# Two hybrid blocks on one core: retention scores one step further behind the rotation, and the gate pieces of two outputs beside the last head

## The reference, cut to what matters

```python
q = rotary(q, positions)
k = rotary(k, positions) * (dk ** -0.5)
...
att = jnp.einsum('bhnd,bhmd->bhnm', qc, kc) * inner_decay
...
mu = jnp.mean(out, axis=-1, keepdims=True)
var = jnp.mean(jnp.square(out - mu), axis=-1, keepdims=True)
out = (out - mu) * lax.rsqrt(var + EPS)
...
y_ret = o_ret.astype(x.dtype) * jax.nn.silu(zr)
merged = jax.nn.sigmoid(ga) * (y_att @ w_proj_attn) + jax.nn.sigmoid(gr) * (y_ret @ w_proj_ret)
return x + gate[:, None, :] * (merged @ w_out)
```

## Time and profile before

| | us |
|---|---|
| median of 3 runs | 3543.75 |
| lowest and highest | 3541.46, 3548.41 |
| the profiled execution's own time | 3547.39 |
| its span | 3545.6 |
| PE busy | 3335.2 (94%) |
| DVE busy | 1714.1 (48%) |
| ACT busy | 1287.0 (36%) |
| POOL busy | 409.7 (12%) |

### The profile page before, as it was taken

The page is one execution under the profiler, slowest core; times in us unless marked ns, Lnnn a source line. Parts: engine busy times, 40 slices in busy tenths (PEclk is TensorE's granted clock), DMA queues, the critical chain, the costliest instruction groups (busy, mean ns, idle before and its releaser), DMA issues.

```text
span 3545.6 us, 42895 instructions
## 1 busy us (share of the span) xinstructions
PE 3335.2 (94%) x17064; PEld 2755.8 (78%) x17064; DVE 1714.1 (48%) x2596; ACT 1287.0 (36%) x1991; POOL 409.7 (12%) x400
## 2 busy tenths in 40 slices
PE   3999998999998999988999999999999999999898
PEld 3788777888887788876888778877778788877686
DVE  3666568655524667676333333343333333433333
ACT  2555533212123656563322333333332333333322
POOL 1111110000001445352000000001200000021100
PEclk7999999999998999999999999999999999999999
DMA  5222224665512111111333322222123222222132
GB/s 178 87 75 81 73 76 135 193 199 185 183 55 69 49 42 48 48 42 63 97 98 97 102 80 71 72 81 74 63 78 98 91 77 72 66 89 78 51 97 85
DMA packets 109286, 318.75 MB, mean 90 GB/s; under 512 B 28192, under 2 KB 30880, under 8 KB 108576
## 3 DMA queue, kind: packets, MB, share of 16 engines
q1 hardware_dynamic: 109088, 316.00, 28.3%
HBM read 313.86 MB, written 2.10 MB: 89 GB/s over the span
## 4 chain that ended last, share of the span: by engine, by line
PE 82%; DVE 7%; ACT 4%; POOL 3%; issue 2%; DMA 1%; SPq 0%; DVEq 0%; ACTq 0%
PE bank L1013 21%; PE bank L1015 20%; PE bank L1014 20%; PE bank L1018 3%; PE bank L1019 3%; PE bank L1020 3%; PE bank L1225 1%; PE bank L1099 1%; DVE tmp L1694 1%; PE bank L1244 1%; PE bank L1109 1%; PE bank L1254 1%; PE bank L1126 1%; ACT L1282 1%; POOL hg_d L2142 1%
## 5 line engine op out<-in xcount | busy, mean ns | idle before, releaser
L1013 PE MATMUL bank<-h_high_lat,w_high 128*128 128x512 f32 x2742 | 1139.8, 416 | 96.4 <-DVE h_low_ctx L1700 34.1
L1642 DVE TENSOR_TENSOR w_low<-w_raw,w_high 128x1024 fp32r<-128x1024 f32 (+3 forms) x442 | 539.8, 1223 | 1135.3 <-ACT w_high L1302 1134.3
L1015 PE MATMUL bank<-h_high_lat,w_low 128*128 128x512 f32 x2742 | 1082.2, 395 | 0.0
L1014 PE MATMUL bank<-h_low_lat,w_high 128*128 128x512 f32 x2742 | 1081.7, 395 | 0.0
L1302 ACT CAST w_high<-w_raw 128x1024 fp32r<-128x1024 f32 (+3 forms) x442 | 451.4, 1022 | 1304.5 <-PE bank L1015 845.7
L1013 PEld LDWEIGHTS bank<-h_high_lat,w_high 128*128 128x128 f32 x2742 | 522.8, 191 | 220.4 <-issue 83.1
L1015 PEld LDWEIGHTS bank<-h_high_lat,w_low 128*128 128x128 f32 x2742 | 522.1, 190 | 113.7
L1014 PEld LDWEIGHTS bank<-h_low_lat,w_high 128*128 128x128 f32 x2742 | 524.4, 191 | 79.5 <-issue 8.3
L2096 POOL TENSOR_TENSOR rstd<-rstd,square 128x512 f32<-128x512 f32 (+1 forms) x42 | 64.8, 1544 | 1456.6 <-ACT square L1283 1455.7
L1018 PE MATMUL bank<-h_high_ctx,w_high 128*128 128x256 f32 x795 | 224.8, 283 | 0.0
L1019 PE MATMUL bank<-h_low_ctx,w_high 128*128 128x256 f32 x795 | 224.7, 283 | 0.0
(11 more groups left out here) (264 smaller groups left out, 4378.9 us busy)
## 6 DMA issues: line engine op xcount, KB each, us to landing
w_raw<-in_w_in_dram SPq DMA_DIRECT2D x176, 512.0 KB, 3.5
w_raw<-in_ada_w_dram SPq DMA_DIRECT2D x88, 512.0 KB, 4.0
w_raw<-in_ffn_in_dram SPq DMA_DIRECT2D x88, 512.0 KB, 3.5
w_raw<-in_w_ada_dram SPq DMA_DIRECT2D x48, 512.0 KB, 4.4
w_raw<-in_hg_in_dram SPq DMA_DIRECT2D x40, 512.0 KB, 3.5
w_raw<-in_ffn_out_dram SPq DMA_DIRECT2D x32, 512.0 KB, 3.5
w_raw<-in_qkv_dram SPq DMA_DIRECT2D x24, 512.0 KB, 3.6
w_raw<-in_proj_ret_dram SPq DMA_DIRECT2D x16, 512.0 KB, 3.5
```

The lines of the kernel that those rows point to most:

```text
L1013: e.matmul(lat_b, a, h[:, k, :], start=start, stop=False)
L1014: e.matmul(lat_b, a, l[:, k, :], start=False, stop=False)
L1015: done = e.matmul(lat_b, b, h[:, k, :], start=False, stop=stop)
L1642: e.tensor_tensor(w_lo[n % 2][:, 0:w], raw[slot][:, 0:w], w_hi[n % 2][:, 0:w].bitcast(F32), ALU.subtract).then_inc(s_lo, 1)
```

## The change

1. `re_mixer` gets an empty step between the rotation and the first scores: 11 steps for 10.
2. The pieces beside the last head are ga(0), gr(0), pa(0), ga(1), gr(1) in 31 slots, with pa(1) behind; before they were ga(0) and gr(0) in 14 slots, with pa(0) behind.
3. In the merge the gates run one output ahead: pr(0), then ga(2), gr(2), pa(2), pr(1), and so on to ga(7), gr(7), pa(7), pr(6), pr(7).
4. `merge_gate` has four buffers for two, and the waits for a free one look one output further back.

```diff
--- before.py
+++ after.py
@@ -394,6 +394,7 @@
             self.ev("re_vt", x, c)
         self.ev("re_rot", x)
         yield
+        yield
         for jt in range(4):
             self.ev("re_sc", x, jt)
             yield
@@ -505,19 +506,20 @@
             first = self.re_mixer(layer, 0)
             start_first = []
             self.interleave([self.at_pieces(layer, j) for j in range(ATT_H)], [(self.at_mixer(layer, j), 7) for j in range(ATT_H)],
-                            10 * (KC - 1), self.re_pieces(layer, 0, lambda: self.start_background(first, 10, 8 * (KC - 1))), 5 * (KC - 1))
+                            10 * (KC - 1), self.re_pieces(layer, 0, lambda: self.start_background(first, 11, 8 * (KC - 1))), 5 * (KC - 1))
             for k in range(ATT_H):
                 self.ev("ya", layer, k)
             self.preload()
             self.ev("re_init", layer)
             self.interleave([self.re_pieces(layer, r) for r in range(1, RET_H)],
-                            [(self.re_mixer(layer, r), 10) for r in range(1, RET_H)], 8 * (KC - 1), self.gate_pieces(layer, 0), 2 * (KC - 1))
+                            [(self.re_mixer(layer, r), 11) for r in range(1, RET_H)], 8 * (KC - 1),
+                            self.gate_pieces(layer, 0) + self.gate_pieces(layer, 1), 4 * (KC - 1) + ATT_H - 1)
             self.preload()
             for k in range(KC):
                 self.ev("yr", layer, k)
             for m in range(KC):
-                if m > 0:
-                    for p in self.gate_pieces(layer, m):
+                if 0 < m < KC - 1:
+                    for p in self.gate_pieces(layer, m + 1):
                         p()
                 self.piece(io["proj_ret"][layer, m], KC, "yr", ("pr", layer, m), gate=("yr", layer) if m == 0 else None)
             for m in range(KC):
@@ -611,7 +613,7 @@
         with ExitStack() as sy:
             YR = sb("y_ret", [P, KC, LAT], F32, sy)
             YAh, YAl = sb("ya_high", [P, ATT_H, LAT], F32R, sy), sb("ya_low", [P, ATT_H, LAT], F32R, sy)
-            gates2 = ring("merge_gate", 2, [P, LAT], sy)
+            gates2 = ring("merge_gate", 4, [P, LAT], sy)
             with ExitStack() as si:
                 head_in = ring("head_in", 14, [P, LAT], si)
                 with ExitStack() as st:
@@ -1417,12 +1419,12 @@
                     elif what == "gate":
                         _, name, layer, m = p.epi
                         g = KC * layer + m
-                        if g > 0 and name == "ga":
-                            e.wait_ge(*lat_free[by_epi[("pa", *divmod(g - 1, KC))]])
-                        elif g > 0:
-                            e.wait_ge(s_ma, g)
+                        if g > 1 and name == "ga":
+                            e.wait_ge(*lat_free[by_epi[("pa", *divmod(g - 2, KC))]])
+                        elif g > 1:
+                            e.wait_ge(s_ma, g - 1)
                         e.wait_ge(s_mm, n + 1)
-                        act(gates2[0 if name == "ga" else 1][:, :], lat_b, ACT.Sigmoid).then_inc(s_la, 1)
+                        act(gates2[2 * (m % 2) + (name == "gr")][:, :], lat_b, ACT.Sigmoid).then_inc(s_la, 1)
                     elif what == "pr":
                         _, layer, m = p.epi
                         e.wait_ge(s_ma, KC * layer + m + 1)
@@ -1777,10 +1779,10 @@
                             e.wait_ge(s_ml, KC * layer + m - 1)
                         e.wait_ge(*lat_free[by_epi[("gate", "ga", layer, m)]])
                         e.wait_ge(s_mm, n + 1)
-                        e.tensor_tensor(tmp[m % 2][:, 0:LAT], gates2[0][:, :], lat_b, ALU.mult).then_inc(s_lv, 1)
+                        e.tensor_tensor(tmp[m % 2][:, 0:LAT], gates2[2 * (m % 2)][:, :], lat_b, ALU.mult).then_inc(s_lv, 1)
                     elif what == "pr":
                         _, layer, m = p.epi
-                        o, g = tmp[m % 2][:, 0:LAT], gates2[1][:, :]
+                        o, g = tmp[m % 2][:, 0:LAT], gates2[2 * (m % 2) + 1][:, :]
                         v = KC * layer + m + 1
                         e.wait_ge(*lat_free[by_epi[("gate", "gr", layer, m)]])
                         e.wait_ge(s_mm, n + 1)
```

## The result

The changed kernel takes 3521.97 us (median of 4 runs, 3519.60 to 3524.94), against 3546.08 for the kernel before in its four runs by then: a ratio of 0.9929, with a 95% interval of 0.9917 to 0.9942. A second set of five runs, with ten of the kernel before beside it, gave 3521.15 and a ratio of 0.9925 (0.9911 to 0.9938). The forecast was 3521.4 and 22.3 us less than the median of the runs shown; the time lies in its range, and faster by more than 0.2% was given 0.94.

The account below looks back on a forecast made before the run. PE, busy for 3335.2 of 3545.6 us, bounds the kernel, so only its waits could shrink. Savings of 11.9 + 4.6 + 1.6 + 4.2 = 22.3 us from 3543.75 gave 3521.4 us, range 3515 to 3529.

Parts of the forecast that it names:

- points 1 and 2: Scores of all retention heads: more matmul groups after DVE's rotation of q shorten PE's waits, 11.9 us saved.
- (3): Scores of the last heads and layer 0's head 0: matmuls no longer at low clock, 4.6 us saved.
- (4): Variance of the last heads: four groups instead of two after the mean end the wait, 1.6 us saved.
- (5): Wait ahead of pr(0): three more groups cover an unchanged chain, 4.2 us saved, a wait of 5.7 us remains.
- Clock behind it: First matmuls of pr(0): low clock after the wait taken as unchanged, zero; at worst 1 us more each.
- the likeness to the wait at the norm: Behind the merge wait: low clock stays, as it came at the norm after 5.99 us without a matmul.
- (6): Merge: gates one output ahead with four buffers add no instructions and looser waits, so zero.
- Rivals A: Scores and merge: the clock gives nothing back, 1 us more behind each merge wait; 15.7 saved, 3528 us, chance 0.12.
- B: Variance and merge: ACT or DVE pass the head's output on later, the merge wait only moves; 3527 us, chance 0.12.
- Rival D: Crossings from pa to pr: weights come late, PE waits 3.0 us at each of 14; slower, 3563 us, chance 0.03.

Follow-up runs that it names:

- the gates alone: The changed kernel without its empty step between rotation and first scores; 3537.59 us, ratio 0.9977 to the kernel before.
- 24 slots: The changed kernel with the last head's 11 steps in 24 slots instead of 31; 3518.70 us, ratio 0.9924 to the kernel before.
- the sigmoid experiment on the kernel before: The kernel before with only the eight casts of y_ret put behind the sigmoid of gr(0); 3539.28 us, ratio 0.9972.
- the one with the sigmoid first: The changed kernel with the eight casts of y_ret put behind the sigmoid of gr(1); 3513.48 us, ratio 0.9907 to the kernel before.
- the version with placed steps: The changed kernel with the last head's steps in hand-named slots, the eight y_ret casts in the last; 3507.49 us, ratio 0.9886 to the kernel before.

## Why the prediction was right

Its terms, with what the two traces of before and after show (us saved over both layers):

| term | forecast | measured | from |
|---|---|---|---|
| waits ahead of the scores | 11.9 | 11.9 | 13.2 less 1.3 |
| clock at the scores | 4.6 | 5.0 | below |
| wait ahead of the variance | 1.6 | 1.6 | 1.6 less 0 |
| merge waits | 4.2 | 4.0 | 15.6 less 11.6 |
| clock behind the merge waits | 0 | -2.0 | below |
| end of a wait itself | not seen | 1.8 | below |
| sum | 22.3 | 22.3 | stretches: 22.5 |

*Scores* (points 1 and 2). Right to a tenth. The empty step alone takes 7.8 of the 11.9 us, the gates alone 2.6; with both, four groups more stand ahead of the last heads' scores. That 0.66 would be left at the last heads was read off heads 1 and 2; it is 0.65 and 0.66.

*Clock at the scores* (3). At the last heads the way from the scores to the second matmul behind them is now 2.02 us in both layers, against 3.72 and 3.63: 1.70 and 1.61. Head 0 of layer 0 gives 1.24 and another 0.42 for matmuls behind that point that were still slow, which the forecast left out.

*Variance* (4). Right, and with it the working: squares ready 2.5 us behind the mean, PE there at 2.8. In the gates experiment the cast and the sigmoid start a group later, which by the same working makes 3.2 for 2.8, and 0.4 was the wait.

*Merge wait* (5). 2.0 each for 2.1. The argument that only the cover changes held because the chain's order was kept. It would not have held for much more cover: ACT's cast of pr(0)'s weights caps it, as 24 slots showed.

*Clock behind it* (5). The one term that was mis-sized. The forecast took 7 slow matmuls behind each wait as unchanged and set 1 us each as the bound. The trace has 12 and 11, for 7 and 6 before; from pr(0)'s start to the 24th matmul behind it 8.08 and 7.93 us pass, for 7.06 and 6.95: 2.0 us lost, the whole bound. The argument that failed was the likeness to the wait at the norm, by which a shorter wait would leave as many slow matmuls behind it. The Trainium skill ("TensorE: Matmul & The Clock Gate", "What's actually happening") says that one kernel showed 6, 11 or 14 slow matmuls, depending on when it started. That is said of a kernel's start; the counts behind the waits here vary too, with 12 and 11, and 14 and 7 behind two equal waits of 3.0 us in the kernel with 24 slots.

*The end of a wait.* What made up for it had not been in the sum. A wait's idle time is counted from the end of a matmul that lasts 0.39 us while its successor would start 0.23 after it, so each wait costs 0.16 more than its bracket; and the scores behind one take 2.02 us to the second matmul, where those without one take 1.95 (2382.93 to 2384.88). That is 0.23 for each of the eight waits that went, six at scores and two at variances. The prediction had no term for it, so that the sum came out to a tenth is luck: 2.0 us lost that it had put at nothing, against 1.8 and 0.4 gained that it had left out. So is a part of the nearness of 3521.97 to 3521.4: the kernel before has a median of 3546.08 over its four runs, 2.3 above the one that the forecast started from, and the first block gave 3.2 us that no term had.

*Gates one ahead, four buffers* (6). No cost found: no wait in the merge beside the old 0.2 us per layer at `m_low`. Rivals A and B named real mechanisms at the wrong place: the clock's loss fell behind the merge wait and not at the scores, and the casts' place on ACT sets the wait once the cover is large enough. Rival D's place shows nothing in the trace after.

## What to carry to other kernels

Where a list spreads a chain over another engine's work, count the groups of work between producer and user: each wait was its chain less its cover, to 0.1 us, until an instruction in the chain itself waited on the cover's end. Then look at what stands in one engine's queue ahead of the instruction that releases the next: one sigmoid moved ahead of eight casts saved some 8 us, a third as much again as the whole change. And price a wait by the clock behind it as well, but as a range.

## What was not expected of the hardware

The low clock does not follow from the length of a wait alone. Ahead of the scores, waits of up to 1.87 us were not followed by it at once in any trace. Of six between 1.95 and 2.03 us five were and one was not; one of 2.7 us was in layer 1 and its twin in layer 0 was not. Ahead of pr(0) there were 7 and 6 slow matmuls after waits of 7.8 us, 8 and 8 after 7.8 in the kernel with the empty step, 12 and 11 after 5.8, 9 and 9 after 5.1, 8 and 8 after 3.4, 14 and 7 after 3.0, none after 1.6 and 1.0. So a shorter wait can cost more in clock than a longer one. PE's timeline of layer 0 in the sigmoid experiment on the kernel before shows how:

```profile
2587.36 0.47 PE L1012 MATMUL bank<-yr_high,w_high 128*128 128x512 f32 x1 [3.40 <-DVE yr_low L2075]
...
2588.60 0.43 PE L1014 MATMUL bank<-yr_high,w_low 128*128 128x512 f32 x1
2588.83 0.62 PE L1012 MATMUL bank<-yr_high,w_high 128*128 128x512 f32 x1
2589.25 0.63 PE L1013 MATMUL bank<-yr_low,w_high 128*128 128x512 f32 x1
...
2591.81 0.59 PE L1013 MATMUL bank<-yr_low,w_high 128*128 128x512 f32 x1
2592.24 0.40 PE L1014 MATMUL bank<-yr_high,w_low 128*128 128x512 f32 x1
```

PE waited 3.40 us, then ran six matmuls at 2.4 GHz (the step from 2588.60 to 2588.83 is 0.23 us), and only then, while busy, fell to 1.2 GHz (0.42 from 2588.83 to 2589.25), for eight. The drop came 1.5 us after the wait had ended. At the longer waits it came inside them, where it costs nothing: over the wait of 7.8 us the granted clock was 0.76 on average in the kernel before, over that of 5.8 us 0.87 in the changed one. With 1.00 and 0.50 as the two levels that makes 3.8 us of low clock inside the wait before and 1.5 after, with 3.1 and 5.3 us of it behind: what the shorter wait no longer held fell on matmuls. This is not the whole of it. With 24 slots the granted clock over the two equal waits was 0.89 and 0.93, so the drop fell in the last 0.7 and 0.4 us of them, and yet 14 matmuls were slow behind the one and 7 behind the other. Why that is so is open.

The kernel before lay between 3541.06 and 3553.45 us in 23 runs, the one with the sigmoid first, which shows no slow matmul at its merge waits, between 3512.29 and 3514.42 in five. These waits do not explain the spread by themselves: the version with placed steps has no slow matmul there either and lay between 3505.81 and 3512.18 in four.
